# The step sizes' product as fp32 matmuls in four column strips, behind the first convolution pair, in a fused two-block network on one core

## The reference

```python
shift, scale, gate = jnp.split(c_act @ ada_w[i] + ada_b[i], 3, axis=-1)
h = _modulate(x, norm_g[i], shift, scale)      # rmsnorm(x) * gain * (1 + scale) + shift
zxbcdt = h @ in_w                              # 5152 columns: z 2048, xbc 3072, dt 32
xbc = jax.nn.silu(_causal_dwconv(xbc, conv_w, conv_b))
dt = jax.nn.softplus(dt + dt_bias)             # step sizes, one per token and head
y = _ssd_chunked(xs, dt, a_neg, bm, cm)
```

## Time and profile before

| | |
|---|---|
| time, median of 3 runs | 1558.29 us (1556.65 to 1560.05) |
| time of the profiled execution | 1557.7 us |
| its span on the core | 1555.8 us |
| TensorE busy | 1540.1 us |
| VectorE busy | 950.0 us |
| ScalarE busy | 678.1 us |
| mean granted clock of TensorE | 0.997 of full speed |

### The profile page before, as it was taken

How to read it: one execution, slowest core, us unless ns; L and a number is a source line. 1 busy time by engine, 2 the same in 40 slices (tenths; PEclk the granted TensorE clock), 3 DMA queues, 4 the chain that set the end, 5 groups by cost and what they waited for, 6 DMA issues and landing times. The chain is left out here.

```text
span 1555.8 us, 19263 instructions
## 1 busy us (share of the span) xinstructions
PE 1540.1 (99%) x7806; PEld 1219.5 (78%) x7806; DVE 950.0 (61%) x1211; ACT 678.1 (44%) x958; POOL 97.4 (6%) x66
## 2 busy tenths in 40 slices
PE   8999999999999999999999999999999999999998
PEld 4788887778788666678898886678888888888887
DVE  4769898996874666755468446754553434432445
ACT  4556567754532655654222455533442222322232
POOL 0000001011300000023000000000120000000110
PEclk8999999999999999999999999999999999999999
DMA  9245334433793111123211122222223222222233
GB/s 389 103 149 176 135 123 135 149 108 139 260 357 108 56 55 46 37 82 111 82 55 55 55 82 95 68 82 89 101 82 108 86 104 99 91 102 102 78 112 122
DMA packets 47383, 177.72 MB, mean 114 GB/s; under 512 B 3616, under 2 KB 20512, under 8 KB 31680
## 3 DMA queue, kind: packets, MB, share of 16 engines
q1 hardware_dynamic: 30368, 167.44, 29.8%
q10 hardware_dynamic: 16928, 9.06, 2.2%
HBM read 172.23 MB, written 4.26 MB: 113 GB/s over the span
## 5 line engine op out<-in xcount | busy, mean ns | idle before, releaser
L658 PE MATMUL bank<-HH,whi 128*128 128x512 f32 x1352 | 556.0, 411 | 0.4 <-issue 0.4
L660 PE MATMUL bank<-HH,wlo 128*128 128x512 f32 x1352 | 528.7, 391 | 0.0
L659 PE MATMUL bank<-HL,whi 128*128 128x512 f32 x1352 | 527.8, 390 | 0.0
L1247 DVE TENSOR_TENSOR wlo<-raw,whi 128x2048 fp32r<-128x2048 f32 (+2 forms) x122 | 267.2, 2190 | 105.8 <-ACT whi L1975 105.0
L658 PEld LDWEIGHTS bank<-HH,whi 128*128 128x128 f32 x1352 | 254.3, 188 | 80.9 <-issue 33.8
L660 PEld LDWEIGHTS bank<-HH,wlo 128*128 128x128 f32 x1352 | 254.1, 188 | 54.8
L659 PEld LDWEIGHTS bank<-HL,whi 128*128 128x128 f32 x1352 | 254.8, 188 | 47.9 <-issue 3.8
L1975 ACT ACTIVATE whi<-raw 128x2048 fp32r<-128x2048 f32 (+2 forms) x118 | 222.5, 1885 | 126.0 <-PE bank L660 108.3
L2577 POOL TENSOR_TENSOR SR<-SR,tmp 128x512 f32<-128x512 f32 x35 | 62.0, 1772 | 596.0 <-ACT tmp L1995 595.0
L1594 DVE TENSOR_TENSOR_SCAN W<-W,cc 128x511 f32<-128x511 f32 (+3 forms) x64 | 49.0, 808 | 34.6 <-ACT W L2310 34.5
L660 PE MATMUL bank<-FH,wlo 128*128 128x512 f32 x176 | 68.5, 389 | 0.0
(11 more groups left out here) (326 smaller groups left out, 2225.6 us busy)
## 6 DMA issues: line engine op xcount, KB each, us to landing
raw<-wstream SPq DMA_DIRECT2D x113, 1024.0 KB, 4.9
aslot<-tstream SPq DMA_DIRECT2D x24, 512.0 KB, 3.6
A<-astream SPq DMA_DIRECT2D x8, 1024.0 KB, 20.4
AC<-scratch ACTq DMA_DIRECT2D x16, 512.0 KB, 5.2
QT<-tstream SPq DMA_DIRECT2D x12, 512.0 KB, 6.9
OZ<-tstream SPq DMA_DIRECT2D x12, 512.0 KB, 8.7
raw<-wstream SPq DMA_DIRECT2D x4, 768.0 KB, 4.9
X<-xT SPq DMA_DIRECT2D x1, 2048.0 KB, 8.3
```

The lines of the kernel that those rows point to most:

```text
L658: e.matmul(o, wh[:, k, c], hi[:, kb0 + k, :], start=first and k == 0, stop=False)
L659: e.matmul(o, wh[:, k, c], lo[:, kb0 + k, :], start=False, stop=False)
L660: x = e.matmul(o, wl[:, k, c], hi[:, kb0 + k, :], start=False, stop=last and k == kb - 1)
L1247: x = e.tensor_tensor(wlo[:, i % 2, c], raw[:, i % 2, c], whi[:, i % 2, c].bitcast(F32), ALU.subtract)
```

## The change

The dt block no longer has a chunk in `weight_plan`. Its 32 columns are appended to the weight stream together with four 32x32 identity matrices, and loaded into `DW` (fp32, 144 KB) on ScalarE's queue. `dt_part(0)` multiplies the blocks k = 0 to 3 of `HH` and of `HL` by it, unsplit, as eight fp32 matmuls with 32 columns of output, each k of four in its own column strip; `dt_part(1)` does k = 4 to 7. ScalarE copies the bank to `DS`, and one more fp32 matmul (`dt_fold`) sums the four strips.

The pair cv 0 and cv 1 is now chunk 0 of the plan. SP starts it behind `A[0]`, and the second chunk behind `A[7]`. The dt block stands third in the ring, behind cv 0 and cv 1. `keep_busy(n)` multiplies a constant by a constant n times (fp32, 256 columns) at three places. `sum_of` stands ahead of `piece(1)` and `high(0)` ahead of `piece_copy(1)`; `high(1)` and `rest(1)` move later.

```diff
--- before.py
+++ after.py
@@ -24,7 +24,7 @@
 
 def weight_plan():
 
-    plan = [(("m_in_w", 0, 8, ((5120, 32), (0, 96))), [("dt", 0)])]
+    plan = []
     for g in range(4):
         plan.append((("m_in_w", 0, 8, ((4096 + 128 * g, 128), (4608 + 128 * g, 128))),
                      [("cv", 6 * g), ("cv", 6 * g + 1)]))
@@ -232,6 +232,8 @@
     ph = ExitStack()
     A = [sbt(f"A{n}", [128, 2048], F32, ph) for n in range(8)]
     AP = [sbt(f"AP{n}", [128, 256], F32, ph) for n in range(2)]
+    DW = sbt("DW", [128, 9, 32], F32, ph)
+    DS = sbt("DS", [128, S], F32, ph)
     ph.close()
     ph = ExitStack()
     Y = sbt("Y", [128, 16, S], F32, ph)
@@ -385,6 +387,9 @@
             if b[0] not in ("pp", "v"):
                 at[b] = len(ring)
                 ring.append(b)
+            if b == ("cv", 1):
+                at["dt", 0] = len(ring)
+                ring.append(("dt", 0))
             if b == ("cv", 2):
                 at["tk", 0] = len(ring)
                 ring.append(("tk", 0))
@@ -397,6 +402,8 @@
             done_at.append((s_ppm, 8 + blocks[-1][1] + 1))
         else:
             done_at.append((s_blk, at[blocks[-1]] + 1))
+
+    dt_weights = wstream[starts[-1]:starts[-1] + 36864].rearrange("(p k n) -> p k n", p=128, k=9)
     blk_done = lambda kind, idx: at[kind, idx] + 1
     bank_of = lambda kind, idx: dense[at[kind, idx] % 3]
 
@@ -501,13 +508,11 @@
         e.dma_start(X[:, :, :], xT).then_inc(l_x, 16)
         for i in range(8):
             ada_first(i)
-            if i == 1:
+            if i == 0:
                 chunk(0)
-            if i == 3:
-                chunk(1)
+        chunk(1)
+        e.dma_start(cbc[:, :], crow.partition_broadcast(128)).then_inc(l_cr, 16)
         chunk(2)
-        e.dma_start(cbc[:, :], crow.partition_broadcast(128)).then_inc(l_cr, 16)
-        chunk(3)
         w.wait_ge(s_mv, 8)
         ada_load(0)
         w.wait_ge(s_acm, 1)
@@ -719,41 +724,72 @@
                              A[i][:, 256 * k:256 * k + 256], start=(k < 4), stop=(k > 3))
             x.then_inc(s_mv, 1)
 
-
-        dt, cv01 = block("dt", 0, "in", 0, 128), both("cv", 0, "in")
-
-        w.wait_ge(s_zero, 1)
+        def dt_part(half):
+
+            w.wait_ge(l_dw, 16)
+            if half == 0:
+                bank_free("dt", 0)
+            ready = h_ready("in")
+            for k in range(4 * half, 4 * half + 4):
+                ready(k)
+            for n, h in enumerate((HH, HL)):
+                for q in range(4):
+                    k = 4 * half + q
+                    x = e.matmul(bank_of("dt", 0)[32 * q:32 * q + 32, :], DW[:, k, :], h[:, k, :].bitcast(F32),
+                                 start=(half == 0 and n == 0), stop=(half == 1 and n == 1))
+            if half == 1:
+                x.then_inc(s_mv, 1)
+
+        def dt_fold():
+
+            w.wait_ge(l_dw, 16)
+            w.wait_ge(s_cp, 9)
+            e.matmul(bank_of("dt", 0)[0:32, :], DW[:, 8, :], DS[:, :], start=True, stop=True).then_inc(s_blk, 1)
+
+
+        cv01 = both("cv", 0, "in")
+
+        def keep_busy(n):
+
+            w.wait_ge(l_con, 16)
+            for i in range(n):
+                e.matmul(bank_of("dt", 0)[:, 0:256], ones, diag[:, 0:256], start=True, stop=True)
+
+
+        w.wait_ge(s_rw, 1)
         for i in range(10):
             e.matmul(aux[0][:, :], zeros[:, 0:128], zeros[:, :], start=True, stop=True)
         piece(0)
+        keep_busy(6)
+        sum_of("x", aux[0])
         piece(1)
-        sum_of("x", aux[0])
         fold(0)
+        keep_busy(1)
         fold(1)
         piece(2)
+        keep_busy(1)
         fold(2)
         piece(3)
+        run(take(cv01, 1))
         fold(3)
-        run(take(dt, 2))
+        run(take(cv01, 1))
         piece(4)
-        run(take(dt, 1))
+        run(take(cv01, 1))
         fold(4)
         run(take(cv01, 1))
         piece(5)
-        run(take(dt, 1))
-        run(take(cv01, 1))
+        dt_part(0)
         fold(5)
         piece(6)
         run(take(cv01, 1))
         fold(6)
         piece(7)
-        run(take(dt, 1))
+        run(take(cv01, 1))
         fold(7)
         run(take(cv01, 1))
-        run(take(dt, 1))
-        run(take(cv01, 1))
-        run(dt)
+        dt_part(1)
         run(cv01)
+        dt_fold()
 
 
         def in_proj(g):
@@ -1256,7 +1292,7 @@
             rest(chunk_of[kind, idx] + 1)
 
 
-        e.memset(zeros, 0.0).then_inc(s_zero, 1)
+        e.memset(zeros, 0.0).then_inc(s_rw, 1)
         e.memset(eps[:, 0:1], EPS)
         e.memset(eps[:, 1:2], EPS * EPS)
         own(e.memset(sel[:, :], 0.0))
@@ -1289,8 +1325,6 @@
             for k in (2 * i, 2 * i + 1):
                 normed("in", k, G1[:, 0:8])
             low_shifted("in", 2 * i, ada[:, 0:8])
-            if i == 1:
-                rest(1)
             low_shifted("in", 2 * i + 1, ada[:, 0:8])
 
         rest(0)
@@ -1298,12 +1332,12 @@
         finish_first(1)
         finish_first(2)
         finish_first(3)
+        rest(1)
 
 
         w.wait_ge(s_blk, blk_done("dt", 0))
         e.tensor_scalar(xb, bank_of("dt", 0)[0:32, :], cv[0:32, VOFF["dtb"][0]:VOFF["dtb"][0] + 1], None,
                         ALU.add).then_inc(s_dtx, 1)
-        rest(2)
         w.wait_ge(s_dte, 1)
         w.wait_ge(s_dtx, 1)
         e.scalar_tensor_tensor(dd, xb, 0.0, dd, ALU.max, ALU.add).then_inc(s_dt, 1)
@@ -2013,6 +2047,7 @@
 
         e.dma_start(cv[:, :], vec).then_inc(l_vec, 16)
         e.dma_start(cc[:, :], con).then_inc(l_con, 16)
+        e.dma_start(DW[:, :, :], dt_weights).then_inc(l_dw, 16)
         w.wait_ge(l_vec, 16)
         e.activation(sg[:, :], vcol("c"), ACT.Sigmoid).then_inc(s_sg, 1)
         lnexp()
@@ -2033,8 +2068,8 @@
         own(e.activation(g2[:, :], vcol("final_g"), ACT.Square))
         own(e.activation(g2[:, :], g2[:, :], ACT.Ln, bias=eps_ap))
         own(e.activation(g2[:, :], g2[:, :], ACT.Exp, scale=0.5))
+        high(0)
         piece_copy(1)
-        high(0)
         w.wait_ge(s_sum, 1)
         rsqrt(aux[0][:, :], D, R[:, :]).then_inc(s_rr, 1)
         piece_copy(2)
@@ -2045,11 +2080,12 @@
                 if i > 0:
                     piece_copy(2 * i + 2)
                 piece_copy(2 * i + 3)
-            if i == 0:
+            if i == 2:
                 high(1)
-
-
-        high(2)
+        w.wait_ge(s_mv, 9)
+        e.activation(DS[:, :], bank_of("dt", 0)[:, :], ACT.Copy).then_inc(s_cp, 1)
+
+
         w.wait_ge(s_dtx, 1)
         w.wait_ge(s_c, 1)
         e.activation(sg[0:32, 0:1], cv[0:32, VOFF["alog"][0]:VOFF["alog"][0] + 1], ACT.Exp)
@@ -2683,6 +2719,8 @@
         w = w[128 * k0:128 * (k0 + kb)]
         w = np.concatenate([w[:, c:c + n] for c, n in cols], axis=1)
         parts.append(w.reshape(kb, 128, -1).transpose(1, 0, 2).reshape(-1))
+    w = a["m_in_w"].reshape(1024, -1)[:, 5120:5152].reshape(8, 128, 32).transpose(1, 0, 2).reshape(128, 256)
+    parts.append(np.concatenate([w, np.tile(np.eye(32, dtype=np.float32), (4, 1))], axis=1).reshape(-1))
     wstream = np.concatenate(parts)
 
     w = a["ada_w"][0][:, 0:2048]
```

More of the change, by code:

```diff
@@ L469, in program @@
     groups = lambda t: t.rearrange("p (s t) -> p s t", t=128)
-    s_zero = sem("s_zero")
+    s_rw, l_dw = sem("s_rw"), sem("l_dw")
     zeros = SR[:, 1, :]
```

## The result

The changed kernel takes 1569.53 us (median of 4 runs, 1568.63 to 1571.48) against 1559.17 us (4 runs), a ratio of 1.0072 with a 95% interval of 1.006 to 1.0084. That is 10.4 us slower, where 8.6 was forecast, and the interval lies clear of no change. The forecast time, 1566.9 us, started from the 1558.29 us of the first three runs of the kernel before; of the 2.6 us between it and 1569.53, some 0.9 is this. The profiled execution took 1570.12 us, with a span of 1568.0 us.

The account below looks back on a forecast made before the run. TensorE, busy 99% of the span, was taken as the bound, so front-stage delays count in full. A 6.2 us later cv 2 plus 2.4 us of clock loss made 8.6 us, giving 1566.9 us; range 1562.5 to 1572.5.

Parts of the forecast that it names:

- The product itself: Step-size product on TensorE: two parts of 1.85 us and a 1.10 us sum, 4.8 us against 5.4, 0.6 saved.
- TensorE's path: Front stage at full clock, waits of 1.85 and 2.85 us ahead of blocks 4 and 6, ending at 51.0 us.
- Moving `high(1)`: ScalarE, in the gap ahead of k = 6: its 1.9 us end before `HH` 6 can start, costing nothing.
- The wait behind it: Ahead of cv 2: a 7.0 us chain until cv 0 is read, starting cv 2 6.2 us later, at 58.1 us.
- the drain: ScalarE's table switch: 1.38 us besides the load by the skill page; not counted, as the rows show none.
- The clock behind the wait: From cv 2 on: TensorE at 1.2 GHz for 4.8 us, half of it lost, 2.4 us; bounds nothing and 2.7.
- the first rival: Front stage: the clock falls in the short waits already, +2 to +4 us, about 1570; chance 0.32.
- the chains through the folds: Front stage: from a pair's second fold to the low part, 3.2 us for the even block, 3.9 for the odd.
- The switches of form: TensorE, front stage: four more switches between dense matmuls and pieces, at most 0.4 us, left out.
- A front stage short enough to make the change no loss: Front stage paced by loads alone: sum of strips at 42.5 us at the earliest, total 1558.3, the same; chance 0.06.

Follow-up runs that it names:

- run 1: Changed kernel with the dt block put back first in the bank ring, TensorE's program order untouched: 1563.57 us.
- run 2: Changed kernel with ScalarE's first readings of cv 0 moved ahead of the work on the step sizes: 1561.77 us.
- x_front: Changed kernel with only the front stage reordered, pieces 6 and 7 and folds 5 and 6 directly behind piece 5: 1563.47 us.
- x_short_fill: Changed kernel with 4 and 6 filler matmuls in the short waits ahead of k = 4 and k = 6: 1567.25 us.
- x_nofill: Changed kernel without its eight filler matmuls, the three calls of `keep_busy` left out: 1574.03 us.
- run 4: Same run as x_front: changed kernel with only the front stage reordered, 1563.47 us.
- x_front_fill: Changed kernel with the front stage reordered and 16 filler matmuls in the long wait ahead of cv 2: 1560.83 us.
- x_fill: Changed kernel with 16 filler matmuls in the long wait behind the sum of strips: 1568.91 us.
- x_front_read: Changed kernel with the front stage reordered and the first readings of cv 0 ahead of the step sizes: 1554.98 us.
- x_front_ring: Changed kernel with the front stage reordered and the dt block first in the bank ring again: 1556.72 us.

## Why the prediction was right, and where a size was off

**The product itself.** `dt_part` takes 34.98 - 33.15 = 1.83 us, the second one 1.86, forecast 1.85. The sum of strips takes 1.05, forecast 1.10. With 4.74 us against 5.44 the product is 0.7 us cheaper.

**TensorE's path.** k = 0 at 24.01 us (forecast 24.35), fold(5) at 34.98 (34.85), waits of 1.87 and 2.87 us ahead of blocks 4 and 6 (1.85 and 2.85). Moving `high(1)` cost nothing, as said: the wait ahead of k = 6 is put down to `HL` and has its forecast length.

**The wait behind it.** 7.16 us, forecast 7.0 from the sum to cv 2, and put down to L2155. The bank order as its cause is shown by run 1, ScalarE's order by run 2. This is the largest term and the mechanism was right. In the changed kernel the table load lasted 1.28 us and the tanh began 0.01 us behind its end (56.69, 57.98), and the drain that the Trainium skill, page ScalarE: Activation LUTs, section What ACT_TABLE_LOAD costs, states does not appear here either. ScalarE's side stayed the shorter, with an idle 0.53 us for `w3h`.

**The clock behind the wait.** Forecast 2.4 us. In the four profiles with an unfilled long wait cv 2 took 8.38 us in the changed kernel (60.98 to 69.36), 6.95 in x_front (54.75 to 61.70), 7.40 in x_short_fill (59.26 to 66.66) and 7.13 in x_nofill (67.48 to 74.61), against 5.63 in the kernel before (51.88 to 57.51). So it loses 1.3 to 2.8 us, and 2.6 between the medians of runs 4 and 5. The mechanism was right. That the size came so near is in part luck: the 4.8 us at half speed came from the step between weight loads at the start of the kernel, where the granted clock of the profile reads 1.00 throughout, and how long TensorE works at half speed differs from execution to execution.

**What was mis-sized: TensorE's path in the front stage.** The step "I follow TensorE through the changed front stage with the durations at full clock" held to within 0.4 us up to 38 us and failed behind that: the sum of strips ended at 53.82 us and not at 51.0. Of these 2.8 us the clock is 1.6. From the start of block 4 to the sum of strips the changed kernel took 52.77 - 38.45 = 14.32 us and x_short_fill, with the clock held, 51.05 - 38.32 = 12.73; the piece at 41.06 us alone took 1.93 us instead of 1.07. This is the first rival, to which I gave 0.32: the clock falls in the short waits already, +2 to +4 us. The other 1.1 us are there at full clock too, since x_short_fill ends its sum at 52.1. They are sums that came out too small: the six matmuls of a block k between two other forms hold TensorE for 1.45 to 1.58 us (39.77 - 38.32, 52.77 - 51.19) where the forecast had 1.36, which makes some 0.7 us with the folds, and the chains through the folds are a little longer than the 3.2 us. The switches of form are part of this. The prediction left them out at 0.4 us; they are indeed some 0.1 us each, but they add up.

By the medians, x_short_fill takes 1567.25 - 1559.33 = 7.9 us more than the kernel before beside it, where the whole forecast was 8.6, and the fall of the clock in the front stage adds 2.3: 10.2 of the 10.4 us measured. So what happened was the forecast's mechanism and the first rival's together. The measured 1569.53 lies nearer to the rival's 1570 than to the forecast's 1566.9, and that it lies within the range owes something to the range's 10 us. Its upper end also counted a drain at the table load, which no run shows.

**The other rivals.** A front stage short enough to make the change no loss: it was not. Its lower limit for the sum of strips, 42.5 us, was not reached in any run; the earliest end is 47.57, in run 4.

## What to carry to other kernels

When a block is moved back in a ring of buffers, ask for each later block whose reader it now waits for, and what stands ahead of that reader on its own engine: here a product that got 0.7 us cheaper brought a wait of 7.2 us, since the neighbour's bank was read behind a chain that the moved product itself starts. A chain that runs under other products costs nothing until it becomes the only thing to do; put its first step early and independent work behind it, as in run 4. And a short wait of TensorE can cost twice, so cheap filler matmuls in waits that can't be removed are worth trying, but they only give back the clock, not the wait.

## What the runs showed of the hardware

- Whether the clock falls behind a wait of 1.9 to 2.9 us differs between executions of the same instructions. In the changed kernel's profile it fell behind the 1.87 us wait (0.50 at 40 us) and not behind the 2.87 us one; in x_read it held behind the first and fell near 48 us behind the second; in x_fill it fell behind both; in x_ring it stayed at 0.50 from 40 to 53 us, across the second wait.
- The scatter of times goes with this. The kernels whose profile shows no fall of the clock and no wait over 1.5 us, x_front_read, x_front_ring and x_front_fill, lie within 0.5 to 0.8 us over 9 or 10 runs. The changed kernel's four runs span 2.9 us, x_ring's five 4.9 and x_nofill's four 5.4.
- Four fp32 products of 32 columns in column strips do run side by side: eight of 512 columns take 1.83 us together (34.98 - 33.15), where one such product takes 1.05 us by itself (L747).
